# A griffin-style decoder layer on one core: forgetting attention by heads with split values stationary, and one merge gate through Exp

## The reference

```python
# A: sparse attention, 8 heads of 64: compressed keys, causal, window of 256   ("NSA")
# B: differential attention, 4 heads: softmax(q1 k1) - lam * softmax(q2 k2),
#    output (512, 4 x 128), rms-normed per head                                ("DIFF")
# C: forgetting attention, 8 heads of 64                                       ("FOX")
s = einsum('bthd,bshd->bhts', qc, k) + Fc[..., :, None] - F[..., None, :]
p = masked_softmax(s, tpos[:, None] >= kpos[None, :])
o_c = einsum('bhts,bshd->bthd', p, v)
gates = sigmoid(mg)
merged = gates[0]*(o_a @ w_br[0]) + gates[1]*(o_b @ w_br[1]) + gates[2]*(o_c @ w_br[2])
h = x + merged @ w_o
out = h + conv_ffn(rms_norm(h))     # up, causal conv of width 3, gelu * gate, down
```

## Time and profile before

| | |
|---|---|
| three runs | 1028.81, 1026.45, 1029.69 us; median 1028.81 |
| profiled execution: time / span | 1028.74 us / 1027.0 us |
| mean granted clock of PE | 0.995 |
| PE busy | 1004.2 us (98%) |
| PEld busy | 844.2 us (82%) |
| DVE busy | 561.5 us (55%) |
| ACT busy | 402.1 us (39%) |
| POOL busy | 95.9 us (9%) |

### The profile page before, as it was taken

The page is one execution under the profiler, slowest core; times in us unless marked ns, Lnnn a source line. Parts: engine busy times, 40 slices in busy tenths (PEclk is TensorE's granted clock), DMA queues, the critical chain, the costliest instruction groups (busy, mean ns, idle before and its releaser), DMA issues.

```text
span 1027.0 us, 13047 instructions
## 1 busy us (share of the span) xinstructions
PE 1004.2 (98%) x5101; PEld 844.2 (82%) x5101; DVE 561.5 (55%) x1035; ACT 402.1 (39%) x729; POOL 95.9 (9%) x84
## 2 busy tenths in 40 slices
PE   6999999999999899999999999999999999999998
PEld 5777889998888677888888888888888888888887
DVE  5746887763565576456555445465655565621213
ACT  5335454534346655424644334342322323212110
POOL 3200000010002000030200031012121112200000
PEclk9999999999999899999999999999999999999999
DMA  6521110102322111232211125222322322322322
GB/s 246 208 80 44 42 43 1 42 1 93 113 82 82 41 42 41 97 109 83 83 42 42 41 82 200 87 82 83 117 89 82 123 82 86 119 82 94 112 83 82
DMA packets 13693, 86.91 MB, mean 85 GB/s; under 512 B 1472, under 2 KB 1984, under 8 KB 4160
## 3 DMA queue, kind: packets, MB, share of 16 engines
q1 hardware_dynamic: 13632, 86.07, 23.7%
HBM read 83.96 MB, written 2.10 MB: 84 GB/s over the span
## 4 chain that ended last, share of the span: by engine, by line
PE 93%; DVE 3%; ACT 3%; issue 1%; DMA 0%; SPq 0%; ACTq 0%; DVEq 0%
PE ps L1277 21%; PE ps L1279 21%; PE ps L1278 21%; PE ps L1455 11%; PE ps L1441 5%; PE ps L1305 4%; PE ps L1427 2%; PE ps L1428 2%; PE ps L1425 1%; PE ps L1332 1%; DVE wl L850 1%; PE ps L1418 1%; PE ps L1358 1%; ACT prob L737 0%; DMA x<-x 0%
## 5 line engine op out<-in xcount | busy, mean ns | idle before, releaser
L850 DVE TENSOR_TENSOR wl<-raw,wh 128x512 fp32r<-128x512 f32 (+2 forms) x118 | 171.7, 1459 | 128.0 <-ACT wh L582 126.6
L582 ACT ACTIVATE wh<-raw 128x2048 fp32r<-128x2048 f32 (+1 forms) x58 | 109.4, 1886 | 152.5 <-PE ps L1279 141.3
L1277 PE MATMUL ps<-aT_h,wh 128*128 128x512 f32 (+1 forms) x376 | 146.8, 390 | 0.9 <-DVE aT_l L859 0.9
L1278 PE MATMUL ps<-aT_l,wh 128*128 128x512 f32 (+1 forms) x376 | 146.4, 389 | 0.0
L1279 PE MATMUL ps<-aT_h,wl 128*128 128x512 f32 (+1 forms) x376 | 146.4, 389 | 0.0
L737 ACT ACTIVATE prob<-ps,nmx 128x384 f32<-128x384 f32 (+3 forms) x128 | 66.6, 520 | 120.5 <-DVE nmx L1048 120.3
L1277 PE MATMUL ps<-wh,aT_h 128*128 128x512 f32 x256 | 102.2, 399 | 0.0
L1279 PE MATMUL ps<-wh,aT_l 128*128 128x512 f32 x256 | 100.1, 391 | 0.0
L1278 PE MATMUL ps<-wl,aT_h 128*128 128x512 f32 x256 | 99.8, 390 | 0.0
L1277 PEld LDWEIGHTS ps<-aT_h,wh 128*128 128x128 f32 (+1 forms) x376 | 70.0, 186 | 16.6 <-issue 1.1
L1279 PEld LDWEIGHTS ps<-aT_h,wl 128*128 128x128 f32 (+1 forms) x376 | 70.0, 186 | 15.4
(11 more groups left out here) (209 smaller groups left out, 1720.6 us busy)
## 6 DMA issues: line engine op xcount, KB each, us to landing
raw<-wblk SPq DMA_DIRECT2D x72, 1024.0 KB, 4.7
x<-x SPq DMA_DIRECT2D x4, 512.0 KB, 5.2
w_sb<-w SPq DMA_DIRECT2D x1, 2048.0 KB, 9.2
hid<-x SPq DMA_DIRECT2D x1, 2048.0 KB, 7.5
out<-outt SPq DMA_DIRECT2D x8, 256.0 KB, 2.0
stage<-consts SPq DMA_DIRECT2D x1, 1216.5 KB, 11.5
later<-consts SPq DMA_DIRECT2D x1, 448.0 KB, 12.2
par<-params SPq DMA_DIRECT2D x1, 204.5 KB, 8.6
```

Source lines behind the costliest of these rows:

```text
L582: nc.scalar.activation(wh[b % 2][:, 0:n], raw[b % RING][:, 0:n], ACT.Copy).then_inc(hi_ready, 4)
L850: ins = nc.vector.tensor_tensor(wl[b % RING][:, cols], raw[b % RING][:, cols], wh[b % 2][:, cols].bitcast(f32), ALU.subtract)
L1277: nc.tensor.matmul(dst, a_h, b_h, start=start, stop=False)
L1278: nc.tensor.matmul(dst, a_h, b_l, start=False, stop=False)
```

## The change

- FOX's units run head by head. Exp writes to one of three `prob_f`; DVE scales it there by the reciprocal sum, before the transposes instead of after the products.
- V is kept as high and low part side by side (`v_hl[t]`, 128 columns a head); ACT writes the high, DVE the low part, and both read the projection's bank.
- The transposed probabilities of all four tiles of a head are collected, high part in `pt_h` by ACT (L778 of the changed kernel), low part in `pt_l` by DVE (L1126), laid out by key block.
- VH: per head eight products with `v_hl` stationary and `pt_h`, then `pt_l`, moving, of 512, 384, 256, 128 columns. The result holds the two halves of V on 128 partitions, transposed already. OH adds the halves (ACT's copy to `otmp`, DVE's sum to `osum`), OS splits a pair of heads into `oT_h` and `oT_l`, for which FOX's first B waits pair by pair. FOX has no O and no OT; the 20 gate steps at its end are in one piece.
- DIFF's gate is exp(-x) on ACT, POOL adds 1, and DVE takes the reciprocal just before the merge product, which multiplies by 2 (the Tanh form was (tanh(x/2)+1)). The preload in SUB is gone.
- DIFF's OT comes two slots later; NSA's first TC comes after four steps of the next gate chunk.
- q's slots are permuted for FOX (`q_slot`), at the same cost; semaphores are declared for all of this.

```diff
@@ -82,7 +82,7 @@
         return [("diff", h, c, i) for i in range(TT) for h in range(4) for c in range(2)]
-    return [("fox", h, 0, i) for i in range(TT) for h in range(8)]
+    return [("fox", h, 0, i) for h in range(8) for i in range(TT)]
@@ -158,25 +158,32 @@
             put(q + t_lag, "A", q)
-            put(q + o_lag, "O", q)
-    for i in range(TT):
+            if m != FOX:
+                put(q + o_lag, "O", q)
+    for h in range(8 if m == FOX else 0):
+        last = TT * h + TT - 1
+        put(last + o_lag, "VH", h)
+        put(last + o_lag + 1, "OH", h)
+        if h % 2:
+            put(last + o_lag + 2, "OS", h // 2)
+    for i in range(TT if m != FOX else 0):
         last = per * (i + 1) - 1 + o_lag
...
             if i < TT - 1:
-                put(last + 3, "OT", i)
+                put(last + 5, "OT", i)
         elif i < TT - 1:
             put(last + 1, "OT", i)
-    order = {k: n for n, k in enumerate(("S", "C", "CN", "TC", "OC", "G", "SC", "A", "O", "SUB", "SUN", "OT", "WL", "W"))}
+    order = {k: n for n, k in enumerate(("S", "C", "CN", "TC", "OC", "G", "SC", "VH", "OH", "OS", "A", "O", "SUB", "SUN", "OT", "WL", "W"))}
     out = [e for j in sorted(at) for e in sorted(at[j], key=lambda e: order[e[0]])]
...
         first = [("G", 0, 8), ("SC", 0), ("W", b, 0), ("G", 8, 16), ("CN", 0), ("WL", b, 0), ("W", b, 1), ("G", 16, 24), ("T", 0), ("WL", b, 1),
-                 ("W", b, 2), ("TC", 0), ("G", 24, 32), ("T", 1), ("WL", b, 2), ("W", b, 3), ("OC", 0), ("WL", b, 3), ("G", 32, head)]
+                 ("W", b, 2), ("G", 24, 28), ("TC", 0), ("G", 28, 32), ("T", 1), ("WL", b, 2), ("W", b, 3), ("OC", 0), ("WL", b, 3), ("G", 32, head)]
     if m == FOX:
-        out += [("G", FILL - tail, FILL - 8), ("OT", TT - 1), ("G", FILL - 8, FILL), ("W", BI[(m, "gate3")] + 2, None), ("WL", BI[(m, "gate3")] + 2, None)]
+        out += [("G", FILL - tail, FILL), ("W", BI[(m, "gate3")] + 2, None), ("WL", BI[(m, "gate3")] + 2, None)]
     else:
@@ -333,6 +342,13 @@
         otok = at("otok", [P, 2, S], f32, RC + 13 * KB)
+        pt_h = at("pt_h", [P, 1920], f32r, RX)
+        pt_l = at("pt_l", [P, 1920], f32r, RX + 6 * KB + 512)
+        otmp = at("otmp", [HD, S], f32, RX + 14 * KB)
+        osum = at("osum", [P, S], f32, RC + 15 * KB)
+        v_hl = [at(f"v_hl{t}", [P, 8, 2, HD], f32r, RA + ((88 + 4 * t) if t < 3 else 48) * KB) for t in range(TT)]
+        prob_f = [at(f"prob_f{n}", [P, S], f32, off) for n, off in enumerate((RA + 52 * KB, RA + 54 * KB, RC + 13 * KB))]
         fT = at("fT", [P, S], f32r, RC + 17 * KB)
@@ -508,10 +526,21 @@
                 h = 2 * h + c
-            return h, h
+            return q_slot(m, h), h
...
             return sum(len(units_of(q)) for q in range(m)) + j
+        def pt_view(t, i):
+            return t[:, P * i:P * i + 384 * (i + 1)].rearrange("p (k c) -> p k c", c=384)[:, :, 0:P]
+        def by_key(t, n):
+            return t[:, 0:n].rearrange("p (k c) -> p k c", c=P)
+        def q_slot(m, h):
+            return h // 2 + 4 * (h % 2) if m == FOX else h
@@ -613,7 +642,12 @@
                             inv_rms(rstd[:, 16 * r:16 * r + 2 * nh], hss[:, 2 * r:2 * r + 2, :].rearrange("p t h -> p (t h)")[:, 0:2 * nh], HD)
-                elif name in ("dv", "fv"):
+                elif name == "fv":
+                    for t in range(TT):
+                        key = ("P", m, name, t)
+                        full(act, key)
+                        nc.scalar.activation(v_hl[t][:, :, 0, :], bank(key)[:, :].rearrange("p (h c) -> p h c", c=HD), ACT.Copy).then_inc(v_hi, 1)
+                elif name == "dv":
                     for t in range(TT):
@@ -734,8 +768,22 @@
                         act.wait_ge(max_ready, unit_no(m, j) + 1)
-                        nc.scalar.activation(prob[:, j % 4, 0:n], ps[b][:, 0:n], ACT.Exp, bias=nmx[:, j:j + 1],
+                        dst = prob_f[j % 3][:, 0:n] if m == FOX else prob[:, j % 4, 0:n]
+                        nc.scalar.activation(dst, ps[b][:, 0:n], ACT.Exp, bias=nmx[:, j:j + 1],
                                              accum_out=lsum[:, j:j + 1]).then_inc(psum_free[b], 1)
+                    elif what == "A" and m == FOX:
+                        s0, n = span(units[j])
+                        b = place[("A", m, j)][0]
+                        full(act, ("A", m, j))
+                        nc.scalar.activation(pt_view(pt_h, j % TT), by_key(ps[b], n), ACT.Copy).then_inc(pt_hi, 1)
+                    elif what == "OH":
+                        full(act, ("OH", j))
+                        if j > 0:
+                            free(act, ("OH", j - 1))
+                        nc.scalar.activation(otmp[:, :], bank(("OH", j))[64:128, :], ACT.Copy).then_inc(o_low, 1)
+                    elif what == "OS":
+                        free(act, ("OH", 2 * j + 1))
+                        nc.scalar.activation(oT_h[:, j, :], osum[:, :], ACT.Copy).then_inc(oT_hi, 1)
                     elif what == "A" and pv_index(m, j) % 2 == 1:
@@ -749,8 +797,11 @@
                                 b = place[("G", m, c)][0]
-                                nc.scalar.activation(gate[:, c, :], ps[b][:, :], ACT.Tanh, scale=0.5).then_inc(psum_free[b], 1)
+                                if m == DIFF:
+                                    nc.scalar.activation(gate[:, c, :], ps[b][:, :], ACT.Exp, scale=-1.0).then_inc(psum_free[b], 1)
+                                else:
+                                    nc.scalar.activation(gate[:, c, :], ps[b][:, :], ACT.Tanh, scale=0.5).then_inc(psum_free[b], 1)
                     elif what == "W":
@@ -766,7 +817,6 @@
                         nc.scalar.activation(sq[:, 0, :], otok[:, j % 2, :], ACT.Square).then_inc(sub_sq, 1)
-                        nc.scalar.preload_act_table_set(LN_EXP)
                     elif what == "SUN":
@@ -883,6 +933,12 @@
                             ins.then_inc(psum_free[b], 1)
+                elif name == "fv":
+                    for t in range(TT):
+                        dve.wait_ge(v_hi, t + 1)
+                        b = place[("P", m, name, t)][0]
+                        nc.vector.tensor_tensor(v_hl[t][:, :, 1, :], ps[b][:, :].rearrange("p (h c) -> p h c", c=HD),
+                                                v_hl[t][:, :, 0, :].bitcast(f32), ALU.subtract).then_inc(psum_free[b], 1)
                 elif name == "cmp":
@@ -1061,6 +1117,23 @@
                                 link(nc.vector.tensor_scalar(coef[:, j:j + 1], rl[:, j:j + 1], gsm[:, i, gi:gi + 1], None, ALU.mult))
+                            else:
+                                p = prob_f[j % 3][:, 0:n]
+                                nc.vector.tensor_scalar(p, p, rl[:, j:j + 1], None, ALU.mult).then_inc(p_scaled, 1)
+                    elif what == "A" and m == FOX:
+                        dve.wait_ge(pt_hi, j + 1)
+                        b = place[("A", m, j)][0]
+                        nc.vector.tensor_tensor(pt_view(pt_l, i), by_key(ps[b], n), pt_view(pt_h, i).bitcast(f32),
+                                                ALU.subtract).then_inc(psum_free[b], 1)
+                    elif what == "OH":
+                        dve.wait_ge(o_low, j + 1)
+                        if j >= 2 and j % 2 == 0:
+                            dve.wait_ge(oT_hi, TT * FOX + j // 2)
+                        b = place[("OH", j)][0]
+                        nc.vector.tensor_tensor(osum[64 * (j % 2):64 * (j % 2) + 64, :], ps[b][0:64, :], otmp[:, :], ALU.add).then_inc(psum_free[b], 1)
+                    elif what == "OS":
+                        dve.wait_ge(oT_hi, TT * FOX + j + 1)
+                        nc.vector.tensor_tensor(oT_l[:, j, :], osum[:, :], oT_h[:, j, :].bitcast(f32), ALU.subtract).then_inc(oT_lo, 1)
                     elif what == "A" and pv_index(m, j) % 2 == 0:
@@ -1073,10 +1146,8 @@
                             nc.vector.scalar_tensor_tensor(dst, ps[b][:, 0:HD], coef[:, j:j + 1], dst, ALU.mult, ALU.add).then_inc(psum_free[b], 1)
-                        elif m == DIFF:
+                        else:
                             nc.vector.tensor_copy(otok[:, i % 2, h * P:(h + 1) * P], ps[b][:, 0:P]).then_inc(psum_free[b], 1)
-                        else:
-                            nc.vector.tensor_scalar(dst, ps[b][:, 0:HD], rl[:, j:j + 1], None, ALU.mult).then_inc(psum_free[b], 1)
                     elif what == "WL":
@@ -1134,7 +1205,12 @@
                         dve.wait_ge(merged_ready, (m - 1) * KD + c - 1)
-                    nc.vector.scalar_tensor_tensor(dst, gate[:, c, :], 1.0, ps[pb][:, :], ALU.add, ALU.mult).then_inc(psum_free[pb], 1)
+                    if m == DIFF:
+                        dve.wait_ge(sig_ready, c + 1)
+                        link(nc.vector.reciprocal(gate[:, c, :], gate[:, c, :]))
+                        nc.vector.scalar_tensor_tensor(dst, gate[:, c, :], 2.0, ps[pb][:, :], ALU.mult, ALU.mult).then_inc(psum_free[pb], 1)
```

(35 more changed lines are left out.)

14 lines of the change are left out of this document (10 added, 4 removed).

## The result

| | kernel before | changed kernel |
|---|---|---|
| median of 12 runs | 1029.22 us | 1030.66 us |
| lowest, highest | 1026.45, 1029.97 | 1028.66, 1032.71 |
| profiled execution: time / span | 1028.74 / 1027.0 us | 1029.55 / 1027.5 us |
| PE, DVE, ACT, POOL busy | 1004.2, 561.5, 402.1, 95.9 us | 994.7, 606.4, 399.1, 112.7 us |

The changed kernel is slower by a ratio of 1.0024, 95% interval 1.0013 to 1.0034, so by 1.3 to 3.5 us (the medians, which both spread over 3 to 4 us, are 1.4 us apart). The forecast was 1028.2 us; the time lies in the range of 1019 to 1037, on the other side of the kernel before than forecast. PE works 9.5 us less and the kernel gains nothing from it.

What follows compares the result with a forecast made beforehand. PE, busy 98% of the span, was taken to bound the kernel. The terms -1.8 -10.6 -5.8 +5.8 +11.9 sum to -0.5 us, so 1028.74 becomes 1028.2 us, range 1019 to 1037.

Steps and rivals of the forecast that it cites:

- NSA's TC: NSA's attention: TC behind four gate steps removes PE's wait for pcT and the drain before it, -1.8 us.
- DIFF's gate by Exp, OT later: DIFF's attention: ten table loads leave ACT and OT moves two slots, closing PE's gaps, -10.6 us (-6 to -11.3).
- FOX, the new ring: FOX's attention: DVE and ACT now wait for each other in every slot, and PE sees +5.8 us (0 to +11).
- FOX, PE work: FOX's attention: old value products and OT removed, 17.2 us, new products added, 11.4 us: -5.8 us (-2.5 to -7).
- DIFF's merge, reciprocal and clock: DIFF's merge: eight DVE reciprocals of 3.35 us delay PE by 10.9 us, plus 1.0 of slower clock: +11.9 us.
- The walk: DIFF's merge, step by step: DVE takes 3.98 us per merge, and PE's waits put it 10.9 us later.
- (b): DIFF's merge: the reciprocal is cheap at 512 elements, no wait in the merge, 1016.3 us; chance 0.08.
- (d): DIFF's merge: the reciprocal is steeper, 4.0 us apiece, eighth bank 5.2 us later, 1033.4 us; chance 0.08.
- the gaps take most of them: DIFF's attention: PE's gaps cover most of 10 us at the lower clock; the rest costs an estimated 2 us.
- (c): FOX's attention: no slack absorbs the weight pieces, +10.9, and products wait for pt_l, +3: 1036.3 us; chance 0.16.
- (a): FOX's attention: the ring stays hidden, +1 instead of +5.8 us, time 1023.4 us; chance 0.22.
- (e): DIFF's attention: the change doesn't reach PE, 4 to 5 us of the gaps stay, 1033 us; chance 0.06.

Runs made afterwards that it cites:

- run 8: The changed kernel with NSA's first TC at its old place: 1032.89 us, ratio to the kernel before 1.0047.
- run 10: The changed kernel, nothing changed, profiled once more: 1031.88 us.
- run 4: The changed kernel with Tanh and the preload back in DIFF's gate, no POOL addition or reciprocal, OT still later: 1026.09 us, ratio to the kernel before 0.9969.
- run 5: The changed kernel with DVE's subtraction for pt_l in FOX behind the next maximum: 1023.68 us, ratio to the kernel before 0.9962.
- Run 1: The kernel before with NSA's moved TC and the whole DIFF part, FOX's attention as before: 1029.71 us, ratio to the kernel before 1.0002.
- run 2: The changed kernel without the eight reciprocals in DIFF's merge, which multiplies by 1+exp(-x): 1020.34 us, ratio to the kernel before 0.9911.
- run 3: The changed kernel with DIFF's sigmoid on ACT alone, without POOL's addition and DVE's reciprocal: 1019.50 us, ratio to the kernel before 0.9905.
- run 7: The changed kernel with DIFF's OT at its old place, two slots earlier: 1032.26 us, ratio to the kernel before 1.0043.
- run 12: The changed kernel, nothing changed, profiled once more: 1028.88 us.

## Why the prediction was wrong on the direction, and which of its mechanisms held

The prediction's sum, term by term, against the first traces:

| term | predicted | trace |
|---|---|---|
| NSA's TC | -1.8 | -1.84 |
| DIFF's gate by Exp, OT later | -10.6 | -9.64 |
| FOX, the new ring | +5.8 | +9.3 (ten gaps between starts of matmuls, beyond the usual distance) |
| FOX, PE work | -5.8 | -8.4 (92.41 less 9.3, against 91.55) |
| DIFF's merge, reciprocal and clock | +11.9 | +11.11 |
| start | 0 | +0.09 |
| sum, FOX's two rows as their +0.86 | -0.5 | +0.58 (spans: +0.54) |

*NSA.* As predicted, and run 8 gives it back.

*The reciprocal.* The price was read from three sizes of the earlier trace rows, 3.35 us; the trace has 3345 ns as the mean of eight:

```profile
L1210 DVE RECIPROCAL gate<-gate 128x512 f32<-128x512 f32 x8 | 26.8, 3345 | 0.0
```

The walk had PE's waits in the merge at 1.2, 1.3, 1.3, 3.4 and 2.5 us with 1.0 for the clock; the trace has gaps of 1.2, 1.1, 1.2, 3.3 and 2.1 beyond a pass's own 0.23, and 1.4 for the clock. The walk's 1.2 us for bank 3 did not come in this trace, because the slow passes took that time; run 10, whose clock fell later, has it with 1.1 and bank 5 with 2.5, as walked. Against the walk's 10.9 + 1.0 that is 1.2 less for bank 3, 0.8 less for the other gaps and 0.4 more for the clock; and the passes right behind a gap, 0.31 us from the next instead of 0.23, with others a little apart, bring back 0.8. So the term was 0.8 us too high, and close in part because these errors cancel. Rivals (b) and (d) are out. Beside it, the estimate from the Trainium skill (VectorE: DVE Perf Modes, section First, the fixed hardware budget) by its repeat count of 8, at a cycle each, was 4.27 us; the trace does not agree.

*DIFF.* Half of the mechanism was right: no ACT_TABLE_LOAD is left between its first and last unit, the waits for `otok` are gone, the wait of 2.0 us for a combined tile is down to 0.5, and ACT's busy time falls by 12.9 us (61.26 to 48.33). But "the exponentials were late by a load in front of them" failed: PE waits 2.4 us for exponentials where it waited 2.2. At the first of these waits DVE stands 1.54 us for `rstd` ahead of the unit's maximum (348.27), the shape of run 4 without its loads; moving that was not tried. So "Ln and Exp now follow the square at once" took away the loads and left DVE's place in the order.

That the term of -10.6 came within 1.0 us of the trace is partly luck. Of the 8.2 us of gaps that it took away only 4.9 went: PE is without an instruction for 3.25 us of the window, before for 8.14. The other 4.75 us lie in PE's busy time, 97.39 instead of 102.14 us for the same 522 instructions, where the prediction had 2 us of slow clock and 0.8 of drains. The kernel before shows where they were:

```profile
352.00:360.00 8.00, 4.47 (x13) 3.48 (x14) 4.33 (x11) 4.27 (x10) 0.00 (x0) 0.63 0.00 0
```

In the 4.9 us behind the first gap (355.1 to 360.0) the granted clock was at its lower level throughout, and from 405.1 to 409.5, behind the last gap, it averaged 0.62. That "the gaps take most of them", as the prediction said of the 10 us at the lower level, was wrong: most of them lay behind the gaps, where PE works.

*FOX.* This is the step that failed by most. "So of 10.9 us PE sees +5.8 us": PE sees 9.3, near the upper end of 11 that I gave the term. I set the ring's average against PE's average, where a late copy is passed on from slot to slot (run 5 takes that away, and with it 6.75 us), and I left out the reading of ACT's accumulator behind each exponential:

```profile
L772 ACT ACTIVATION_READ_ACCUMULATOR prob_f<-ps,nmx 128x1 f32 x32 | 6.2, 193 | 0.0
```

That is 0.8 us a head on ACT. On DVE the same stage shows how much it stands for ACT, 14.9 us for `pt_h` and 7.6 for `otmp`, where the earlier trace rows had it standing for PE alone:

```profile
L1126 DVE TENSOR_TENSOR pt_l<-ps,pt_h 128x128 fp32r<-128x128 f32 (+3 forms) x32 | 15.6, 488 | 15.0 <-ACT pt_h L778 14.9
...
L1133 DVE TENSOR_TENSOR osum<-ps,otmp 64x512 f32<-64x512 f32 x8 | 5.5, 684 | 7.6 <-ACT otmp L783 7.6
```

The ring's price was thus 3.5 us too low; how much of it is the reading of the accumulator no run separates. PE's saving was too low by 2.6 us and hid most of that. The products take 1.33 us a head (in the rows of run 5, 0.66 from 518.23 to 518.89, and 0.67 to the next start at 519.56) where I had 1.43, since the last product of four is not held for the 0.105 us of a weight load that I took (0.06 between starts), and the waits break the queue for less than 0.08. The larger part is the transposes, whose cost I had carried over unchanged. The kernel before, then the changed one:

```profile
567.63 0.60 PE L1305 MATMUL ps<-ident,prob 128*128 128x128 f32 x4
568.07 1.00 PE L1441 MATMUL ps<-V,probT 128*128 128x64 f32 x8
```

```profile
525.42 0.60 PE L1385 MATMUL ps<-ident,prob_f 128*128 128x128 f32 x4
525.77 0.42 PE L1498 MATMUL ps<-fT,sel 128*128 128x384 f32 x1
```

Four transposes took 0.44 us with a float32 product behind them, and take 0.35 with a score behind them; in the kernel before the four of `otok`, with a score behind them, took 0.36. No run tests the successor as the cause. Over ten blocks of eight heads the transposes' distances sum to 8.6 us before and 6.6 now. Run 5 shows the saving without most of the ring: 85.66 us, 5.9 below before.

*The direction.* The three gains and the two new waits nearly cancel, as the sum said; the terms' errors of 1.0 (DIFF), 0.9 (FOX, net) and -0.8 us (merge) and 0.1 at the start turn -0.5 into the trace's +0.5. The runs have 1.4 (medians) to 2.5 us (ratio). Run 1, with the new merge and the old FOX, is at 1.0002, so by the ratios most of it comes with FOX's form. The sum put at nothing what its gaps do to the clock, although it had 1.0 us of slow clock behind the merge's gap: where the first wait of 2.0 us is followed by 1.2 GHz, as in four of the eight traces that have this wait, the stage takes another 1.3 us. That makes +0.9 or +2.2 us for FOX. The first trace had the full clock there, so the comparison by terms above doesn't contain it. The merge may lose another 1.5 us (run 10). How often either happens in runs without a profile stays open.

*The rivals.* (c), "the ring binds in full", had the right direction of the error, but not its size: it had 13.9 us for the ring (5.8 and its 8.1), the trace has 9.3, a little nearer to the forecast. Its waits for `pt_l` are waits for `pt_h` in the trace, 5.8 us in five of them. (a) is out, by the waits in FOX. (e), "the loads were not what made DVE and ACT late", came to 1.0 of its 5 us by the time; by the gaps it had more: 3.25 of 8.14 us stay, and the clock made up for that.

## What to carry to other kernels

A function that costs a table load on one engine can cost more as arithmetic on another: ln and exp in the loaded table set made the same sigmoid for 8.8 us of hidden ACT time, where DVE's reciprocals took 26.8 us at the one place where banks wait for DVE. When a cross-engine step is added to a slot, write down each engine's order and look for a cycle; here moving one subtraction behind the next maximum was worth 6.75 us, with not one instruction fewer. And where a sum of large terms comes near zero, its sign is no forecast: give the cancelling terms' errors, not the sum's.

## What was not expected of the hardware

- RECIPROCAL on DVE is linear from 8 to 512 elements a partition: 204, 753 and 3345 ns for 8, 96 and 512, so 6.2 ns an element, against 687 ns for a product of 512 that also reads PSUM.
- The same wait of 2.0 us in FOX is followed by 1.2 GHz in the runs 2, 3, 8 and 10 and by full clock in the first trace and in the runs 4, 7 and 12. A stop of PE has a price of its own beside its length, here 1.3 to 1.5 us, and in FOX it is not paid each time.
- POOL's merged addition, 1.29 us, takes 3.27 us in both places of this merge where it runs beside DVE's split of a block of 2048, and still 1.29 beside a reciprocal of 3.35 us:

```profile
441.12 1.29 POOL L1335 TENSOR_TENSOR merged<-merged,bt 128x512 f32<-128x512 f32 x1 [2.70 <-DVE bt L1211]
445.11 3.27 POOL L1335 TENSOR_TENSOR merged<-merged,bt 128x512 f32<-128x512 f32 x1 [2.69 <-DVE bt L1211]
```
